# A stage's modulation products taken two weight pieces at a time, in four groups of 32 output partitions

## The reference, cut to what matters

```python
mod_ctx = (jax.nn.silu(c_ctx) @ w_ada[l] + b_ada[l])[None, None, :]
mod_lat = (jax.nn.silu(c) @ w_ada[l] + b_ada[l])[:, None, :]
...
sh1, sc1, g1, sh2, sc2, g2 = jnp.split(mod, 6, axis=-1)
h = x * (1.0 + sc1) + sh1
p = h @ w_in
...
x = layer_norm(ALPHA * x + g1 * mix, ln1_g, ln1_b)
h = x * (1.0 + sc2) + sh2
x = layer_norm(ALPHA * x + g2 * peer_ffn(h, peer_wq, peer_subkeys, peer_u, peer_v), ln2_g, ln2_b)
```

## Time and profile before

| | before |
|---|---|
| median of 3 runs | 3798.97 us (3793.69 to 3815.99) |
| profiled execution, its own time | 3786.59 us |
| its span, first to last instruction | 3784.8 us |
| `begin` and the barrier behind it | 0 to 147.97 us |
| mean granted TensorE clock | 0.911 |

### The profile page before, as it was taken

One profiled execution on the slowest core, in us unless ns is written; L12 is line 12 of the kernel. 1 busy time (PEld: TensorE's weight loads), 2 busy tenths in 40 slices (PEclk: granted clock), 3 DMA queues, 4 the chain that ended last, 5 costly groups with the idle time before them and its releaser, 6 DMA issues. The chain is left out here.

```text
span 3784.8 us, 36035 instructions
## 1 busy us (share of the span) xinstructions
PE 2815.2 (74%) x11910; PEld 1705.7 (45%) x11910; DVE 1900.5 (50%) x4344; ACT 939.5 (25%) x2376; POOL 1599.5 (42%) x1578
## 2 busy tenths in 40 slices
PE   8787797874777888888758769969377677777775
PEld 3585586771222333333227658859322222222221
DVE  1114655588744444444452355557485444444445
ACT  2334443331111111111123344334211111111111
POOL 0001000006777777777720100000077777777774
PEclk9897798887999999999979779979589999999998
DMA  9856476657999999999975547656799999999996
GB/s 391 323 196 197 139 246 232 242 201 283 375 407 410 410 411 410 410 409 407 409 276 195 185 158 255 230 220 213 264 367 360 408 409 407 409 409 406 408 408 257
DMA packets 323465, 1206.55 MB, mean 319 GB/s; under 512 B 39370, under 2 KB 41930, under 8 KB 311250
## 3 DMA queue, kind: packets, MB, share of 16 engines
q0 software_dynamic: 221184, 805.40, 54.0%
q10 hardware_dynamic: 75328, 274.86, 20.6%
q1 hardware_dynamic: 26772, 123.99, 8.6%
HBM read 1061.47 MB, written 142.64 MB: 318 GB/s over the span
## 5 line engine op out<-in xcount | busy, mean ns | idle before, releaser
L1822 PE MATMUL acc<-exp_uv,exp_diag 128*128 128x512 f32 x3072 | 1458.0, 621 | 609.3 <-ACT exp_diag L1791 609.2
L1691 DVE CUSTOM_DVE_ANT_0 exp_uv<-exp_uv,h_tok 128x1024 f32<-128x1024 f32 x768 | 940.9, 1226 | 986.9 <-DMA exp_uv<-u_rows,exp_eid 985.4
L1658 POOL DMA_INDIRECT exp_uv<-u_rows,exp_eid x768 | 789.9, 1029 | 1270.3 <-DVE exp_eid L1766 1004.4
L1822 PEld LDWEIGHTS acc<-exp_uv,exp_diag 128*128 128x128 f32 x3072 | 576.3, 197 | 1479.4 <-issue 1479.3
L1658 POOL DMA_INDIRECT exp_uv<-in_v,exp_eid x768 | 771.1, 1004 | 234.2 <-issue 234.2
L1800 ACT ACTIVATE exp_gel<-exp_dot 128x2 f32<-128x2 f32 x384 | 78.1, 203 | 1717.9 <-DVE exp_dot L1691 1717.8
L268 ACT COPY rows<-rows_bank 128x512 f32<-128x512 f32 x512 | 277.4, 588 | 371.4 <-PE rows_bank L253 316.0
L253 PE MATMUL rows_bank<-ident,rows 128*128 128x128 f32 x2048 | 308.0, 300 | 74.7 <-ACT rows L268 74.6
L253 PEld LDWEIGHTS rows_bank<-ident,rows 128*128 128x128 f32 x2048 | 255.1, 154 | 123.6 <-issue 121.4
L1791 ACT ACTIVATE exp_diag<-ident,exp_w 128x128 f32<-128x128 f32 x768 | 260.0, 386 | 0.0
L517 PE MATMUL project_bank<-project_hs,project_ws 128*128 128x384 f32 x960 | 187.9, 353 | 29.4 <-DVE project_hs L505 29.4
(11 more groups left out here) (296 smaller groups left out, 2589.1 us busy)
## 6 DMA issues: line engine op xcount, KB each, us to landing
rows<-in_u ACTq DMA_DIRECT2D x256, 512.0 KB, 5.8
u_rows<-rows ACTq DMA_DIRECT2D x256, 512.0 KB, 5.2
ring<-in_w_ada SPq DMA_DIRECT2D x48, 1024.0 KB, 8.0
ring<-in_w_in SPq DMA_DIRECT2D x20, 1024.0 KB, 8.0
ring<-in_wq SPq DMA_DIRECT2D x16, 1024.0 KB, 7.2
exp_uv<-u_rows,exp_eid POOLq DMA_INDIRECT x768, 6.6
exp_uv<-in_v,exp_eid POOLq DMA_INDIRECT x768, 6.6
ring<-in_w_out SPq DMA_DIRECT2D x8, 1024.0 KB, 13.2
```

The lines of the kernel that those rows point to most:

```text
L1658: nc.gpsimd.indirect_dma_start(buffer_of(n)[:, half * D:half * D + D], None, table, bass.IndirectOffsetOnAxis(eid[:, t, k:k + 1], 0)).then ...
L1691: V.tensor_tensor_reduce(buffer_of(n)[:, 0:D], buffer_of(n)[:, 0:D], h_tok[:, t, :], 1.0, 0.0, ALU.mult, ALU.add, dot[:, j % 8, n % G:n % ...
L1822: ins = nc.tensor.matmul(acc[2 * t + h][:, :], diag[:, n % DIAGS, :], buffer_of(n)[:, D + 512 * h:D + 512 * h + 512], start=(k == 0), stop ...
```

## The change

In `begin` two pieces are taken together. `ada_pair_product` waits for both, makes four products of the bias row and 8 x 4 products of 128 columns each: quarters 0 and 1 come from the first piece, 2 and 3 from the second, and quarter q writes PSUM partitions 32q and 32q + 1, columns 0 to 127, of one bank. The stationary operand is the same for all. `ada_pair_copy` takes the four quarters with four copies. SyncE waits for a pair's product before it refills either slot. Table rows begin behind pair 3 and come two behind each pair. The same product of the next layer, made in `experts`, stays as it was.

```diff
+PAIR = 2
+QUARTER = 2 * NW_ADA // 4
...
+def ada_quarters(rows, m, q):
+    return rows[:, (PAIR * m) * NW_ADA + q * QUARTER:(PAIR * m) * NW_ADA + (q + 1) * QUARTER]
+def ada_pair_product(c, s, pe, rows, piece_full, m):
+    b, r = s.steps.at("ada", m)
+    for n in range(PAIR * m, PAIR * m + PAIR):
+        pe.wait_ge(piece_full[slot(n)], filled(n))
+    pe.wait_ge(s.free[b], r)
+    w = [c.ring[:, slot(n), :].rearrange("p (k n) -> p k n", k=KD) for n in range(PAIR * m, PAIR * m + PAIR)]
+    outs = [s.bank[b][32 * q:32 * q + 2, 0:QUARTER] for q in range(4)]
+    for q in range(4):
+        c.nc.tensor.matmul(outs[q], c.ones[:, :], ada_quarters(rows, m, q)[0:1], start=True, stop=False)
+    for k in range(KD):
+        for q in range(4):
+            ins = c.nc.tensor.matmul(outs[q], c.silu[:, k, :], w[q // 2][:, k, (q % 2) * QUARTER:(q % 2 + 1) * QUARTER],
+                                     start=False, stop=(k == KD - 1))
+    ins.then_inc(s.full[b], 1)
+def ada_pair_copy(c, s, act, rows, m):
+    b, r = s.steps.at("ada", m)
+    act.wait_ge(s.full[b], r + 1)
+    for q in range(4):
+        ins = c.nc.scalar.copy(ada_quarters(rows, m, q), s.bank[b][32 * q:32 * q + 2, 0:QUARTER])
+    ins.then_inc(s.free[b], 1)
...
-def ada_transposes(c, s, pe, rows):
+def ada_transposes(c, s, pe, rows, per=1):
...
-    for n in range(N_ADA):
+    for n in range(N_ADA // per):
...
-        b, r = s.steps.at("ada", (8, 20)[which] + n)
+        b, r = s.steps.at("ada", ((8, 20)[which] + n) // per)
...
-        turns = [("ada", n) for n in range(N_ADA)] + [("cols",)]
+        turns = [("ada", m) for m in range(N_ADA // PAIR)] + [("cols",)]
...
                     if n >= SLOTS:
-                        b, r = s.steps.at("ada", n - SLOTS)
+                        b, r = s.steps.at("ada", (n - SLOTS) // PAIR)
                         sp.wait_ge(s.full[b], r + 1)
...
-                    ada_copy(c, s, act, rows, t)
-                for n in range(TILES, N_ADA):
-                    ada_copy(c, s, act, rows, n)
-                    rows_act(c, act, IN_BEGIN)
+                    ada_pair_copy(c, s, act, rows, t)
+                for m in range(TILES, N_ADA // PAIR):
+                    ada_pair_copy(c, s, act, rows, m)
+                    rows_act(c, act, PAIR * IN_BEGIN)
...
-                for n in range(N_ADA):
-                    ada_product(c, s, pe, rows, piece_full[slot(n)], filled(n), slot(n), n)
-                    if n >= TILES:
-                        rows_pe(c, pe, IN_BEGIN)
-                ada_transposes(c, s, pe, rows)
+                for m in range(N_ADA // PAIR):
+                    ada_pair_product(c, s, pe, rows, piece_full, m)
+                    if m >= TILES:
+                        rows_pe(c, pe, PAIR * IN_BEGIN)
+                ada_transposes(c, s, pe, rows, PAIR)
```

More of the change, by code:

```diff
@@ L189, in ada_columns, with store_gate @@
     c.nc.vector.tensor_scalar(c.mod_cols[:, 1::2], cols[:, 1::2], 1.0, None, ALU.add).then_inc(s.free[b], 1)
-def store_gate(c, s, act, rows, which, place, stored):
+def store_gate(c, s, act, rows, which, place, stored, per=1):
     for n in range(N_GATE2):
-        b, r = s.steps.at("ada", (8, 20)[which] + n)
+        b, r = s.steps.at("ada", ((8, 20)[which] + n) // per)
         act.wait_ge(s.free[b], r + 1)
@@ L331, in _ @@
                 for which, q in enumerate((2, 5)):
-                    store_gate(c, s, act, rows[:, q * D:(q + 1) * D], which, c.gate_dram[0, which], S["gates_stored"])
+                    store_gate(c, s, act, rows[:, q * D:(q + 1) * D], which, c.gate_dram[0, which], S["gates_stored"], PAIR)
                 b, r = s.steps.at("cols")
```

## The result

The changed kernel took 3792.28 us (median of 20 runs, 3777.05 to 3803.55), the kernel before 3801.39 us (20 runs). The ratio is 0.9975 with a 95% interval of 0.9963 to 0.9987: 9.5 us faster, 5 to 14. A second series (12 runs) gave 0.9978 [0.9964, 0.9991]. Forecast were 3794 us, 5 us faster. The profiled execution of after took 3795.4 us, span 3793.6 us; that of before took 3786.6, less than any of the 20 timed runs, so the two spans must not be subtracted.

A forecast was written before the change was run, and what follows sets the result against it. In the first stage TensorE set the pace, only just ahead of nearly full DMA queues. 7 us gained there and 1.7 lost in scoring give -5 us: 3794 us on the median of 3799.0, range 3780 to 3810.

The forecast's parts named there:

- What is late next: First stage: the DMA keeps the beat at 10.16 us a pair; TensorE's saved 1.5 us becomes waits for weight pieces.
- The stage gains bytes: First stage: 18 table rows instead of 21, 3.1 MB less to move, ending 7 us earlier (3 to 11).
- What comes back later: Scoring stage: the three missing table rows are made there, behind its last query products, costing 1.7 us (0 to 2.6).
- The cost of a product: First stage, TensorE: a pair's 72 instructions at 68 ns each take 4.9 us instead of 8.1.
- What would show it: Profile signs: 72 instructions in 4.5 to 5.5 us, TensorE awaiting pieces, beat about 10.1 us, next stage at about 141.
- The rival of the clock: First stage: idle TensorE drops to half clock, two rows take 1.8 us longer, 10.5 us a pair, 3797 us; chance 0.10.
- The rival of groups that do not overlap: First stage: column groups do not overlap, TensorE paces at 11.9 us a pair, +15 us, 3814 us; chance 0.10.
- No change: First stage: paired requests or late stores of x eat the DMA's gain; -1 to +3 us, 3800 us; chance 0.17.
- More gain: First stage's queues exceed 413 GB/s (-3) and scoring hides its rows (-1.7); about -11 us, 3788 us; chance 0.08.

## Why the prediction was right, and where not

The measured median, 3792.3 us, lies 2 us from the 3794 forecast, but that is a weak test and in part luck: the range of 30 us would have held no change as well, and the timed gain is 9.5 us (5 to 14) where 5 were forecast. The marks in the traces test the mechanism better.

- *What is late next* held. The beat forecast was 10.16 us, it is 10.2 to 10.4, the queues are full at 401 GB/s, and TensorE's saving bought nothing in it. Six buffers moved the wait and did not shorten the stage.
- *The stage gains bytes* held: 7 us forecast, 7.2 measured, and putting the three rows back took 6.0 of them away. That 7.2 lies so near is luck too: against the second trace of before it is 10.3. Two parts of the sum were off. The stores of x were to be issued 5.2 us behind the last product; they were issued 7.9 to 9.1 behind it (13.6 and more in the second trace), because ScalarE waits for the stores of table rows ahead of them. And the first pairs were to come every 5.1 us; they came 6 to 10 us apart in the two traces, since the sum counted only the weights: up to 37 us ScalarE's queue brought 4.8 MB of table rows, x and normalisation data beside 9.0 MB on SyncE's.
- *What comes back later* held: 1.7 us forecast in the scoring stage, 1.8 measured (4.3 earlier at its first scores, 2.5 at VectorE's last part). I held the stages between unchanged, but 2.9 us of the gain went there (7.2 at the start of the projection, 4.3 at the first scores). Of the signs of being wrong this is the one that came. 1.4 us of it lie in the first query product, in both traces of either kernel (7.13 and 7.12 us after, 5.75 and 5.74 before); it starts at a granted clock of 0.50, which lasts for its first 2.6 us before and for 4.2 us after. The projection lost 1.8 us in one trace of after and 0.2 in the other; that too may be the clock, which was not tried. The two products, first before and then after:

```profile
736.44 5.75 PE L517 MATMUL score_bank<-score_xs,score_ws 128*128 128x384 f32 x24 [3.23 <-DVE score_xs L505]
```

```profile
730.80 7.13 PE L552 MATMUL score_bank<-score_xs,score_ws 128*128 128x384 f32 x24 [3.42 <-DVE score_xs L540]
```

- *The cost of a product* was mis-sized. I took 68 ns an instruction from 32 tiny transposes as a floor for issuing, 4.9 us a pair. It is 56 ns at the lower clock (3.60 us for 64), and at the full clock 30 ns: in the kernel with six buffers, and for one pair of the changed kernel too, it took 1.93 us in a stretch with the clock at 1.00. The stretch of the changed kernel's product in the windows, columns as in the earlier trace rows, then the timeline and the stretch with six buffers:

```profile
62.50:66.00 3.50, 3.50 (x56) 0.50 1.01 414
```

```profile
59.92 0.40 PE L187 MATMUL begin_bank<-begin_rows,ones 1*2 1x128 f32 x8 [0.35 <-issue]
60.25 1.93 PE L190 MATMUL begin_bank<-ring,cond_silu 128*2 128x128 f32 x64
```

```profile
59.90:62.20 2.30, 2.25 (x72) 1.00 1.04 433
```

  With its bias products a pair takes 2.3 us at the full clock, near the 2.0 that I had worked out for full overlap, and the tiny transposes were no floor. It cost the forecast nothing, because TensorE was not the bound.
- *What would show it* was wrong in two lines. A pair's 72 instructions were to take 4.5 to 5.5 us; they take 4.1 at the lower clock and 2.3 at the full one. And I expected TensorE to wait for weight pieces. It waits for ScalarE, and ScalarE for stores of table rows; the six buffers fit the reading that this ring of buffers is the shallowest on the full queues.
- *The rival of the clock* came true as a mechanism (0.74 granted, a table row at 1.94 us) and not in its price: I added 1.8 us a beat to TensorE's 8.7, but the products took 3.6 and not 4.9, so that the beat stayed the queues'. The Trainium skill (TensorE: Matmul & The Clock Gate, HAM oscillation) says that waits for DMA between bursts bring the half clock. The trace agrees: 0.74 here against 1.00 before, with waits that the profile books to ScalarE, which itself waits for stores.
- *The rival of groups that do not overlap* was priced at +15 us against the kernel before. The kernel with one group lies above it by 5.2 us at the next stage and 10.1 at the first gather (2.1 and 6.7 against the second trace of before): the price was too high, because its beat is 10.51 us and not 11.9. Against the changed kernel both marks moved by 12.4.
- *No change* is excluded by both intervals. *More gain* is not excluded by the time: its price, about 11 us, lies inside 5 to 14 (its own terms, -5, -3 and -1.7, add up to about 10). Its mechanism did not show: the beats did not fall to 9.9 us, and the scoring stage did not hide its rows.
- The Trainium skill's rule on evacuation (TensorEngine Tiling (Array Packing), PSUM Bottleneck) did not bind: four copies take 1.05 us a pair (0.25 and 0.80 in the trace), on an engine that waits 54.5 us for stores in the stage.

What stays open is size. The marks give 2.4 and 3.3 us at the first gather against the first trace of before and 5.7 and 6.6 against the second, on average 4.5, near the 5 that were forecast; the two series of timed runs give 9.5 (5 to 14) and 8 (3 to 14). The two agree within their spreads, but the traces do not show where more than 4.5 would come from; the expert stage varies by 7 to 15 us between traces of one kernel and cannot tell.

## What to carry to other kernels

When a profile shows an engine and the DMA queues both full, work out the bytes per beat before making the engine faster: here a product that became up to 3.7 times as fast bought 1 to 2 us, too little for single traces to tell from nothing, and 3 MB less to move bought 6. The faster product paid only after the table rows had moved to a stage with free queues: there the next stage started at 122 us with the old product, at 106 with pairs in four groups, and at 94 with single pieces in two. Taking two pieces together halves the lookahead of a ring of four, and with it the queues stood at 330 of 413 GB/s; how much of that the lower clock caused was not tried. The output groups need no second piece: two groups of half a piece's columns take twice as long as four groups of quarters, and that was still fast enough to wait for its pieces.

## What the runs showed of the hardware that was not expected

- Products with 2 stationary columns and 128 moving ones, float32, all 128 rows contracted: 112 ns an instruction in one output group (7.15 us for 64), 60 in two (1.92 for 32), 30 in four (1.93 for 64), at the full clock. Four groups are 3.7 times as fast as one. Whether 30 ns is a floor, no run shows.
- At the lower clock (granted 0.50) the same 64 instructions in four groups take 3.60 us, 56 ns each, and 32 in two groups 3.58 us, 112 ns each: both 1.9 times the figures at the full clock.
- At the same place TensorE waited 1.64 us in one trace of before and 1.96 in the other. Behind the first wait the granted clock was 1.00, behind the second 0.50, which cost the stage 3 us.
- With both queues loaded a table row of 0.5 MB took 8.2 us to store with three buffers in the kernel before, 13.9 in the changed one and 19.2 with six buffers, at the same rate (400, 397 and 400 GB/s).
